# Packing narrow weight tiles: eight tiles of 96 columns become six of 128, and the squares of two norms go partly to PSUM

## The reference

```python
# end of the first block
x = x + peer_ffn(rmsnorm(x, norm2_g), ...)          # experts
x = rmsnorm(x, normf_g)                             # norm 3 of the kernel
# second block
h = rms_norm(x, norm_mix)                           # norm 4 of the kernel
z = h @ w_in     # z_rnn (768), z_q (384), z_k (384), z_v, z_g, z_dec (16), z_mq (768), z_gate
xr = causal_dwconv(z_rnn, rnn_conv_w, rnn_conv_b)   # width 4, then a gated recurrence (RG-LRU)
...                                                 # chunked gated linear attention on z_q, z_k, z_v
m = rms_norm(mem, mem_norm)
mk, mv = split(m @ w_mem_kv)                        # 768 columns each
s = einsum(mq, mk) * 192 ** -0.5; out_c = softmax(s) @ mv
```

## Time and profile before

| | |
|---|---|
| median of 3 runs | 1739.05 us (1738.14 to 1739.81) |
| the profiled execution, its time | 1740.4 us |
| its span | 1738.7 us |
| PE busy | 1686.0 us (97%) |
| DVE, ACT, POOL busy | 1044.3, 887.4, 902.8 us |

### The profile page before, as it was taken

The page is one execution under the profiler, slowest core; times in us unless marked ns, Lnnn a source line. Parts: engine busy times, 40 slices in busy tenths (PEclk is TensorE's granted clock), DMA queues, the critical chain, the costliest instruction groups (busy, mean ns, idle before and its releaser), DMA issues.

```text
span 1738.7 us, 34206 instructions
## 1 busy us (share of the span) xinstructions
PE 1686.0 (97%) x13029; PEld 1579.8 (91%) x13029; DVE 1044.3 (60%) x1801; ACT 887.4 (51%) x1174; POOL 902.8 (52%) x398
## 2 busy tenths in 40 slices
PE   8998899999999999999999999989999999899997
PEld 7997899899999999988888888889989999799997
DVE  5996755259922777778888666767335272543422
ACT  4555665455565444444444455544566444466652
POOL 7785368668885000000000444556755688678885
PEclk9999999999999999999999999999999999999999
DMA  5554235455556555555556666544433345455553
GB/s 178 170 183 133 85 120 173 146 171 181 183 179 190 163 167 168 161 166 169 171 178 192 195 193 186 179 124 127 147 115 92 118 140 156 151 159 182 185 186 111
DMA packets 79321, 277.03 MB, mean 159 GB/s; under 512 B 8784, under 2 KB 11136, under 8 KB 79232
## 3 DMA queue, kind: packets, MB, share of 16 engines
q1 hardware_dynamic: 78736, 274.15, 50.4%
q0 software_dynamic: 496, 1.66, 0.3%
HBM read 274.73 MB, written 1.05 MB: 159 GB/s over the span
## 4 chain that ended last, share of the span: by engine, by line
PE 88%; DVE 6%; issue 2%; POOL 2%; ACT 2%; DMA 0%; SPq 0%; DVEq 0%; ACTq 0%; POOLq 0%
PE gemm L589 35%; PE gemm L838 20%; PE gemm L594 17%; PE aux L1085 4%; PE gemm L657 3%; PE aux L814 2%; POOL w_lo L436 2%; PE gemm L621 1%; DVE big L1621 1%; PE gemm L610 1%; DVE big L1652 1%; ACT w_hi L1140 0%; DVE big L1766 0%; PE aux L783 0%; PE aux L938 0%
## 5 line engine op out<-in xcount | busy, mean ns | idle before, releaser
L436 POOL TENSOR_TENSOR w_lo<-raw,w_hi 128x1024 fp32r<-128x1024 f32 (+2 forms) x372 | 889.4, 2398 | 418.3 <-ACT w_hi L1140 382.9
L1140 ACT ACTIVATE w_hi<-raw 128x1024 fp32r<-128x1024 f32 (+2 forms) x532 | 553.7, 1044 | 684.2 <-PE gemm L589 349.2
L589 PE MATMUL gemm<-h_lo,w_hi 128*128 128x256 f32 (+1 forms) x2368 | 333.0, 283 | 0.4 <-DVE mem_lo L1667 0.4
L589 PE MATMUL gemm<-h_hi,w_hi 128*128 128x256 f32 (+1 forms) x2304 | 331.4, 287 | 1.3 <-PE aux L783 0.7
L594 PE MATMUL gemm<-h_hi,w_lo 128*128 128x256 f32 (+1 forms) x2304 | 323.6, 283 | 0.6 <-POOL w_lo L436 0.6
L589 PEld LDWEIGHTS gemm<-h_lo,w_hi 128*128 128x128 f32 (+1 forms) x2368 | 304.9, 189 | 1.0 <-DVE mem_lo L1667 0.9
L589 PEld LDWEIGHTS gemm<-h_hi,w_hi 128*128 128x128 f32 (+1 forms) x2304 | 297.9, 190 | 4.4 <-issue 2.8
L594 PEld LDWEIGHTS gemm<-h_hi,w_lo 128*128 128x128 f32 (+1 forms) x2304 | 295.8, 189 | 1.7 <-POOL w_lo L436 1.4
L436 DVE TENSOR_TENSOR w_lo<-raw,w_hi 128x1024 fp32r<-128x1024 f32 x160 | 195.3, 1222 | 115.5 <-ACT w_hi L1140 112.9
L838 PE MATMUL gemm<-w_hi,h_hi 128*128 128x512 f32 x1024 | 256.7, 393 | 0.0
L838 PEld LDWEIGHTS gemm<-w_hi,h_hi 128*128 128x128 f32 x1024 | 189.8, 188 | 38.2
(11 more groups left out here) (348 smaller groups left out, 1932.8 us busy)
## 6 DMA issues: line engine op xcount, KB each, us to landing
raw<-in_w_u SPq DMA_DIRECT2D x128, 512.0 KB, 3.5
raw<-in_w_ev SPq DMA_DIRECT2D x128, 512.0 KB, 3.8
raw<-in_w_up SPq DMA_DIRECT2D x48, 512.0 KB, 3.8
raw<-in_w_gate SPq DMA_DIRECT2D x24, 512.0 KB, 3.6
raw<-in_w_down SPq DMA_DIRECT2D x24, 512.0 KB, 3.5
raw<-in_w_branch SPq DMA_DIRECT2D x24, 384.0 KB, 3.4
raw<-in_w_conv_in SPq DMA_DIRECT2D x16, 512.0 KB, 4.3
raw<-in_w_peer_q SPq DMA_DIRECT2D x16, 512.0 KB, 4.3
```

What stands on the lines that cost most here:

```text
L436: eng.tensor_tensor(w_lo[v][0:rows, 0:n], raw[c.raw][v][0:rows, 0:n], w_hi[v][0:rows, 0:n], ALU.subtract).then_inc(lo_ready[v], 1)
L589: mm = pe.matmul(out, w[:, k, :], act_part[:, k, :], start=(n == k == 0), stop=False)
L1140: act.activation(w_hi[v][0:rows, 0:n], raw[c.raw][v][0:rows, 0:n], ACT.Copy).then_inc(hi_ready[v], 1)
```

## The change

Sections mem_k, z_rnn and zmq go from 8 tiles of 96 columns to 6 of 128, and zq and zk together (8 tiles) become one section zqk of 6. The weights in memory stay as they were: tiles of 96 columns. SP loads six of the eight as before, and the last two into a buffer `spare`; columns 32*j to 32*j+31 of a spare tile become columns 96 to 127 of a packed tile. ACT rounds such a tile in two instructions (96 columns from `raw`, 32 from `spare`), POOL subtracts in two, PE multiplies with 128 columns, and ACT empties a bank in three (`evacuate_packed`): 96 partitions by 512 to their place, and twice 32 partitions by 256 to the blocks 6 and 7.

In the memory stage sum_squares(3) stands behind mem_k's fourth tile of six, sum_squares(4) behind mem_v's second of six. The squares of norms 3 and 4 are taken in halves, the even slice to SBUF, the odd one to PSUM banks (`squares_psum`), so that DVE's pair addition reads one operand from PSUM; `1/std` of these norms also goes to PSUM, and the scaling reads it there. ACT rounds one tile, not two, before the squares of norm 3. The three small DMAs go from POOL to SP behind mem_k's loads, and POOL's wait for x2_done comes behind the mem_k subtractions. In zmq the six tiles stand before the gate products of h = 0, 1, 2, 4, 5, 6.

```diff
-    section("mem_k", 4)
+    section("mem_k", 3)
-    section("z_rnn", 4)
+    section("z_rnn", 3)
-    for name, count in (("zq", 2), ("zk", 2), ("zv", 3), ("zmq", 4), ...
+    for name, count in (("zqk", 3), ("zv", 3), ("zmq", 3), ...
@@ subtract (POOL)
+                if c.index in packed:
+                    hi, lo = by_k(w_hi[v], P), by_k(w_lo[v], P)
+                    eng.tensor_tensor(lo[:, :, 0:C96], by_k(raw[c.raw][v], C96), hi[:, :, 0:C96], ALU.subtract)
+                    eng.tensor_tensor(lo[:, :, C96:P], spare_columns(packed[c.index][1] + v), hi[:, :, C96:P],
+                                      ALU.subtract).then_inc(lo_ready[v], 1)
+                    continue
@@ sync
+            def load_packed(name, c, v, n):
+                s = PACKED.index(name)
+                if n % 3 == 0:
+                    if s:
+                        last = plan[PACKED[s - 1]][(n + 2) // 2]
+                        sp.wait_ge(lo_ready[n % 2], last.split + 1)
+                    sp.dma_start(spare[:, n // 3].rearrange("p k m -> p (k m)"),
+                                 packed_source(name, 6 + n // 3)).then_inc(spare_in[n // 3], 16)
+                load(c, v, packed_source(name, n))
...
+                if name == "mem_k":
+                    sp.wait_ge(x2_done, BANKS)
+                    sp.dma_start(rwa, ...); sp.dma_start(rwx, ...); sp.dma_start(wdec, ...)
@@ gpsimd
-            pool.wait_ge(x2_done, BANKS)
-            pool.dma_start(rwa, ...); pool.dma_start(rwx, ...); pool.dma_start(wdec, ...)
-            pool.memset(zr[:, :, 0:RNN_CONV - 1], 0.0).then_inc(pads2, 1)
             for c in plan["mem_k"][1:]:
                 subtract(pool, c, n=floats[c.index])
+            pool.wait_ge(x2_done, BANKS)
+            pool.memset(zr[:, :, 0:RNN_CONV - 1], 0.0).then_inc(pads2, 1)
@@ tensor
-                if i == 1:
-                    sum_squares(3)
-                if i == 3:
-                    sum_squares(4)
-            for c in plan["mem_v"]:
+                if i == 1:
+                    sum_squares(3, bank=aux[0])
+            for i, c in enumerate(plan["mem_v"]):
                 by_token(c, (h_lo, mem_lo))
+                if i == 0:
+                    sum_squares(4, bank=aux[0])
@@ round_tile (ACT)
+                if c.index in packed:
+                    s, n = packed[c.index]
+                    hi = by_k(w_hi[v], P)
+                    act.activation(hi[:, :, 0:C96], by_k(raw[c.raw][v], C96), ACT.Copy)
+                    act.wait_ge(spare_in[(n + v) // 3], 16 * (s + 1))
+                    act.activation(hi[:, :, C96:P], spare_columns(n + v), ACT.Copy).then_inc(hi_ready[v], 1)
+                    return
@@ ACT
+            def evacuate_packed(c, dst, spilled):
+                n, bank = packed[c.index][1], pair(gemm[c.bank])
+                look_ahead(c.index + 1)
+                taken(act, c)
+                act.activation(dst, bank[0:C96], ACT.Copy)
+                for v in range(2):
+                    block, j = divmod(n + v, 3)
+                    ins = act.activation(spilled[j * SPILL:(j + 1) * SPILL, block], bank[C96:P, v, :], ACT.Copy)
+                ins.then_inc(evacuated[c.bank], 1)
...
+            look_ahead(mem_k[1].index, 1)
+            def squares_psum(ready):
+                act.activation(root[:, :], epsc[:, :], ACT.Sqrt)
+                for n in range(4):
+                    ready(n)
+                    act.activation(sq[:, 2 * n, :], xres[:, 2 * n, :], ACT.Square)
+                    act.activation(aux[n][:, 0:T], xres[:, 2 * n + 1, :], ACT.Square).then_inc(squared, 1)
+            squares_psum(lambda n: act.wait_ge(x2_done, n + 1))
+            for i in range(2):
+                evacuate_packed(mem_k[i], mk[:, 2 * i:2 * i + 2, :], mk[:, 6:8])
+            deviation(3, aux[0])
+            look_ahead(mem_v[0].index)
+            squares_psum(lambda n: act.wait_ge(normed, 2) if n == 0 else None)
+            evacuate_packed(mem_k[2], mk[:, 4:6, :], mk[:, 6:8])
+            look_ahead(mem_v[1].index)
+            taken(act, mem_v[0])
+            act.activation(mv[:, :, 0:CW], pair(gemm[mem_v[0].bank]), ACT.Copy).then_inc(evacuated[mem_v[0].bank], 1)
+            deviation(4, aux[0])
+            look_ahead(mem_v[2].index, 1)
+            round_h(2)
@@ DVE
+            def pair_psum(i, n):
+                dve.wait_ge(squared, 4 * i + n + 1)
+                dve.tensor_tensor(sq[:, 2 * n, :], sq[:, 2 * n, :], aux[n][:, 0:T], ALU.add).then_inc(paired, 1)
-            normalise(3, xres, xres, "normf_g")
+            normalise(3, xres, xres, "normf_g", inverse=aux[1][:, 0:T])
-            normalise_split(4, 2, "norm_mix_2")
+            normalise_split(4, 2, "norm_mix_2", inverse=aux[1][:, 0:T])
```

More of the change, by code:

```diff
@@ L356, in build @@
         landed = [[sem(f"landed{r}{v}") for v in range(2)] for r in range(RAW)]
+        spare_in = [sem(f"spare_in{n}") for n in range(2)]
         hi_ready = [sem(f"hi_ready{v}") for v in range(2)]
@@ L437, in subtract, with packed_source, spare_columns @@
                                   ALU.subtract).then_inc(lo_ready[v], 1)
-        NARROW = {name: KD * C96 for name in ("mem_k", "z_rnn", "zq", "zk", "zg", "zmq")}
+        NARROW = {name: KD * C96 for name in ("zg",)}
+        PACKED = ("mem_k", "z_rnn", "zqk", "zmq")
+        SPILL = P - C96
+        packed = {c.index: (s, 2 * i) for s, name in enumerate(PACKED) for i, c in enumerate(plan[name])}
+        def packed_source(name, n):
+            if name == "zqk":
+                name, n = ("zq", n) if n < GH else ("zk", n - GH)
+            return t[f"w_{name}"][n]
+        def spare_columns(n):
+            return spare[:, n // 3, :, n % 3 * SPILL:(n % 3 + 1) * SPILL]
         floats = {c.index: NARROW.get(name, TILE) for name, chunks in plan.items() for c in chunks}
@@ L1369, in _, with mem_values_out @@
                                ACT.Copy).then_inc(experts_moved[1], 1)
-            look_ahead(plan["mem_k"][0].index + 1)
-            squares(xres, ready=lambda n: act.wait_ge(x2_done, n + 1))
-            mem_k = plan["mem_k"]
-            for i, c in enumerate(mem_k):
-                evacuate(c, mk[:, 2 * i:2 * i + 2, :], pair(gemm[c.bank], C96))
-                if i == 1:
-                    deviation(3)
-                    look_ahead(mem_k[3].index)
-                    act.wait_ge(normed, 2)
-                    squares(xres)
-                if i == 3:
-                    deviation(4)
-                    look_ahead(plan["mem_v"][0].index, 1)
-                    round_h(2)
-            for i, c in enumerate(plan["mem_v"]):
-                evacuate(c, mv[:, :, i * CW:(i + 1) * CW], pair(gemm[c.bank]))
+            mem_k, mem_v = plan["mem_k"], plan["mem_v"]
+            look_ahead(mem_k[1].index, 1)
[12 more added lines that the diff above has]
+            evacuate_packed(mem_k[2], mk[:, 4:6, :], mk[:, 6:8])
+            def mem_values_out(i):
+                evacuate(mem_v[i], mv[:, :, i * CW:(i + 1) * CW], pair(gemm[mem_v[i].bank]))
+            look_ahead(mem_v[1].index)
[4 more added lines that the diff above has]
+            round_h(2)
+            mem_values_out(1)
+            mem_values_out(2)
             act.wait_ge(lam_abs, 1)
@@ L1413, in _ @@
             for h in range(K96):
-                if h % 2 == 0:
-                    c = plan["zmq"][h // 2]
-                    evacuate(c, mq[:, h:h + 2, :], pair(gemm[c.bank], C96))
+                if h in MQ_TILES and MQ_TILES.index(h) % 2:
+                    i = MQ_TILES.index(h) // 2
+                    evacuate_packed(plan["zmq"][i], mq[:, 2 * i:2 * i + 2, :], mq[:, 6:8, :])
                 act.wait_ge(rg_psum, h + 1)
@@ L2059, in gla_decayed @@
             def gla_decayed():
[L2061 removed]
+                moved(dve, plan["zqk"])
                 dve.wait_ge(gla_exp, 3)
```

65 lines of the change are left out of this document (35 added, 30 removed).

## The result

The changed kernel takes 1715.49 us (median of 4 runs, 1712.65 to 1718.43), the kernel before in the same comparison 1739.43: ratio 0.9863, 95% interval 0.9845 to 0.9881. It is faster by 24 us; the prediction was 1713.4 and a gain of 25.7. The profiled execution took 1715.97 (span 1714.0). It lies 24.4 under the 1740.4 on which the sum was made.

The account below looks back on a forecast made before the run. PE, busy 97% of the span, was taken as the bound. 15.0 - 2.2 + 5.2 + 5.5 - 2.6 + 5.2 - 0.4 = 25.7 us off 1740.4 gave 1714.7, less 1.35 for the median: 1713.4, range 1708.5 to 1721.5.

Parts of the forecast that it names:

- own signs of being wrong: POOL's piece above 1.0, L2027 over 6 us late, or POOL or DVE kept out longer than one piece.
- Memory stage: From first mem_k tile to h_lo: earlier norms and fewer tiles cut 54.1 to 39.1 us, 15.0 off.
- Rival B: Memory-stage norms stay late because PSUM reads do not free DVE: 15.0 becomes 10.6, time 1718; chance 0.10.
- Splitting: POOL's extra 256-column piece per packed tile: taken as 0.67 us, barely hidden; cost 0, up to 3.6.
- Rival A: POOL becomes the bound through its quarter piece: about 1720 at 1.2 us each, near 1737 at 1.81; chance 0.13.
- z_rnn, first product: End of mem_v to z_rnn's next tile: late rounding and POOL pieces make 6.9 into 9.1, 2.2 lost (1 to 4).
- zqk: The merged zq and zk section: 22.9 becomes 17.4 us, 5.5 off, with POOL catching up during dec.
- zv: DVE's convolution ends late, so ACT holds up PE around zv's fourth tile: 2.6 us lost (0 to 5).
- the attention: Its start: ACT comes 0.4 us later against PE, with more to empty before the last gates; 0.4 lost.
- Rival C: Starvation in the convolution: DVE's two-operand steps held through several POOL pieces, slower, 1771; decides from 1.9 us a step; chance 0.02.
- Rival D: No change in time: the edits only shift stalls, losing all 21.9 us of the tiles; chance 0.01.
- rival E: Better: no wait in zv (2.6) and z_rnn's first product nearly as before (1.8): 1709; chance 0.12.

Follow-up runs that it names:

- e2: Kernel before with the norm part alone (squares and 1/std partly in PSUM, new order of work), no packed tiles: 1730.80 us, ratio 0.9955.
- e8: Changed kernel with the norms' squares all in SBUF and only 1/std in PSUM: 1715.50 us, ratio 0.9866.
- e1: Changed kernel with the norms' squares and 1/std all in SBUF, order of work kept: 1719.98 us, ratio 0.9894.
- e6: Changed kernel with DVE's first lambda step moved ahead of the fourth norm: 1712.13 us, ratio 0.9851.
- e4: Changed kernel with DVE's z_rnn convolution accumulating in PSUM, PE's gate products waiting for the whole convolution: 1713.20 us, ratio 0.9852.
- e10: Changed kernel with two more DVE steps, adding zero times the input, in the convolution's third group alone: 1712.54 us, ratio 0.9847.
- c1: The changed kernel run once more, unaltered, on one chip beside a better version: 1717.37 us, ratio 0.9876.
- e3: Changed kernel with the norm part undone, packed tiles kept: 1726.19 us, ratio 0.9925.
- e5: Changed kernel with every DVE convolution step waiting for the one just before it, operands still in SBUF: 1713.60 us, ratio 0.9854.
- e9: Changed kernel with two more DVE steps, adding zero times the input, in each group of the convolution: 1717.95 us (one run).

## Why the prediction was right, and where it was not

The forecast's case came, and its time was 2.1 us low. Of its own signs of being wrong, two came all the same: a piece of POOL's above 1.0, and an engine kept out for longer than one piece. By its steps:

**Memory stage, 15.0 forecast, 14.3 measured.** The times on the way came within 0.5 us, one within 1.1 (forecast in brackets): additions done at 1137.0 (near 1137), sum at 1142.7 (1143.2), deviation 1144.7 (1144.7), scaling done at 1150.2 (1150.1), h_hi whole at 1164.0 (1162.9), mem_v's last tile rounded from 1163.9 (1163.9). e2 has the norms' half of it by itself, 8.8 of stage. Right, with one qualification: the argument that a PSUM operand frees DVE was made for additions and scalings alike; e8 shows that only the scalings needed it. Rival B, that reads from PSUM don't free DVE, is refuted by e8 beside e1. Its price was too low as well: the norms late cost 6.1 us, not 4.4.

**Splitting, a quarter piece of 0.67 taken.** All 24 of them, by source line in the changed kernel (shortest, median, longest in ns):

```profile
L444 POOL TENSOR_TENSOR w_lo<-big,w_hi x24: 727/746/3150, 1128.3 to 1252.5; 128x256 fp32r<-128x256 f32 x24
```

Right for most, but four are above 1.0. The longest is the held one; 1.71 (at 1128.3) lies beside one long DVE operation with two SBUF operands, `mem_lo` of 2.9 us, and 1.19 (at 1172.2) beside the h_lo subtractions; the fourth is 1.12 (at 1234.6). Rival A, with 1.2 or more for each, did not come. The Trainium skill's charge for small read commands (GPSIMD Engine Reference, "Performance pitfalls for Q7 kernels"), which the prediction set beside it, is not seen in these pieces of eight runs: 1.85 and 0.75, the medians of the two pieces, are 0.2 more than the 2.4 of a whole tile, where the estimate had 1.4.

**z_rnn, first product, 2.2 lost forecast, 1.4 measured,** in three waits of PE: 0.54 and 0.55 for w_hi in the rows above and 0.57 for h_lo; a fourth, 0.38 for w_lo, lies in the rest, as forecast. e6 shows that 0.7 of it, and 0.3 behind it, was ACT's wait for the lambda step, which the prediction had put at 1.1 in all.

**zqk, 5.5 forecast, 1.7 measured: the step that failed.** It was "POOL may fall behind by 0.2 a tile, yet it begins 1.5 early and catches up ... Cost 0; up to 3.6 if the piece takes 1.0". POOL did not fall behind gradually. One piece was held for 2.4 us, PE waited 2.02, and the clock fell from 2.4 to 1.2 GHz behind the gap: from 1198.66 on, two groups of eight took 1.72 and 1.69 from start to start for 0.96, so 1.5 us more. The bound was near in size, the mechanism was another: I counted contention as DVE being late and POOL losing at most 0.3 for a step let through, from the earlier trace rows, and took the 5.83 us of the earlier trace rows as the one danger, in which DVE is held through three pieces. It goes the other way as well. e4 shows that the two SBUF operands do it, e10 that the hold is not of fixed length, and c1, e1, e3 and e8 have the held piece again at the same place. That the bound of 3.6 met the 3.8 lost is luck: it was counted from slower pieces, and 1.5 of the 3.8 are the clock, which e1 did not lose.

**zv, 2.6 lost forecast, nothing measured.** The count "one step for each POOL piece, two a tile" took DVE for the loser each time. In dec and in the run above DVE went ahead unhindered, the convolution ended at 1206.5 and not near 1217, and L2104 had 11.67 us to spare. The mechanism itself is there: e5, where DVE is the loser throughout, ends its steps at 1215.9, about 1 us late, for nothing; e9 ends them 5.1 us late and pays 3.2 in zv. The forecast's lateness of 4.4 lay between them.

**zmq 5.3 for 5.2, the rest of z_rnn 4.9 for 5.2, the attention 0.4 for 0.4, the tiles as counted.** The two large misses cancel in part: zqk 3.8 too good, zv 2.6 too bad. That, and not the working of each step, is why the total came within 1 us of its own sum, 25.7 against 24.7. The other 1.1 us lie in the level of the runs against the one profiled.

Rival C (starvation, slower) did not come: where DVE was the loser throughout (e5), its 32 steps took 1.12 us on the mean (1180.25 to 1215.97, 1.45 in the two slowest groups), under the 1.9 from which it decides. Rival D did not come either. Of rival E the half about zv came (no wait there), and the time did not.

## What to carry to other kernels

Where DVE and POOL both work from SBUF, put one operand of each long DVE series in PSUM, and find the one that lies beside POOL's work first: here a single operand, 1/std, was worth 6.1 us of stage and 4.5 in the medians, and the squares nothing. Count a hold in both directions, over several of the other engine's instructions (six here), and place it against the one piece that the critical engine waits for next. Test the halves of a change by themselves: the tiles' gain in the memory stage was worth less without the norms' (3.7 of 5.5).

## What the runs showed of the hardware that was not expected

- A 256-column subtraction of POOL, 0.73 us undisturbed, took 3.15 while six DVE steps with two SBUF operands ran 0.40 us apart, and 2.24 over four; a 768-column one took 4.19 for 1.85. Which engine is held does not follow from the order of the starts: with the same 0.11 us between them POOL lost at 1194.5 and DVE at 1182.6. The Trainium skill (SBUF — State Buffer, "Who interferes with whom") has the engine that issued first hold the shared ports for its whole instruction, with the other blocked. The traces agree that the steps which read two tensors meet POOL only when both lie in SBUF (e4, e1 beside e8). They disagree on the length: here it was several instructions of DVE's (3.15 us), and in the earlier trace rows several of POOL's (5.83 us). In the changed kernel, e6 and e10 the record of the held piece starts about 0.1 us ahead of the run of DVE that holds it, so by the records POOL's had started first.
- Steps that read one tensor are not free of POOL: in the changed kernel the second L2092 of the third group, from SBUF to SBUF, took 2.08 us beside the piece of 1192.56, and 0.40 with no piece beside it.
- Two instructions that did nothing for the result came with a zqk stage 2.4 us shorter (18.82 for 21.23): 0.9 less of PE's wait, 1.5 less of half clock.
- The granted clock differs between executions of one kernel, far from the change. From 1370 to 1400 us it was 1.00 in the first profile of the changed kernel and 0.89 in the second (c1). c1 was 1.4 us ahead of the first profile before that, 0.9 behind in it, and level afterwards. e4, with 0.89 too, had its lead of 4.9 us fall to 2.4 and come back to 3.2. Its gain of 3.8 us in a stage showed as 2.3 us between the medians; the stage in the trace tells more than the time. The window of c1:

```profile
1370.00:1400.00 30.00, 27.16 (x206) 26.96 (x205) 23.03 (x13) 13.98 (x16) 23.17 (x9) 0.89 0.42 123
```
